# Three products of constants left out of the routing stage of a two-layer decoder kernel

## The chip, the core and the metric

The kernel runs on one core of a Trainium2 chip. The metric is device microseconds (us) of one execution, from the runs shown below; lower is better. TensorE is the matmul engine (PE in the profile, and PEld for its weight loads), VectorE is DVE, ScalarE is ACT, GpSimd is POOL, and SyncE (SP) issues most of the transfers.

## The reference

Two decoder layers on 256 tokens of width 1024, all in float32. Layer 0 has sparse attention over keys that an indexer picks, then a dense SwiGLU. Layer 1 has stick-breaking attention, then a mixture of experts: each token goes to the best two of eight experts. Only the last part bears on this case:

```python
def moe_ffn(u, router_w, w_gate_up, w_down):
    B, S, D = u.shape
    tok = u.reshape(B * S, D)
    logits = (tok @ router_w).astype(jnp.float32)
    top_vals, top_idx = lax.top_k(logits, TOP_K_EXPERTS)          # 2 of 8
    gates = jax.nn.softmax(top_vals, axis=-1)
    dense_gates = jnp.sum(jax.nn.one_hot(top_idx, N_EXPERTS, dtype=jnp.float32) * gates[..., None], axis=1)
    y = jnp.zeros_like(tok)
    for e in range(N_EXPERTS):
        y = y + dense_gates[:, e:e + 1].astype(tok.dtype) * swiglu(tok, w_gate_up[e], w_down[e])
    return y.reshape(B, S, D)
```

## The kernel before

Each engine has its own program, written out by hand in order, and the engines meet at semaphores; there is no planner. The first 408 us of the profiled execution hold layer 0, the shared keys and values and the attention of layer 1. Their products are made in three passes of split operands (`product`, whose matmuls are on lines 530 to 532). Then comes the routing stage, from about 408 to 425 us, and after it the expert stage until the end.

The routing stage is a chain between TensorE, VectorE and ScalarE. TensorE transposes the residual stream `h` (`stream_T`, line 863) and multiplies it by the router's weights (`router_product`, line 870: weights of 8 columns, 128 moving columns). The logits are copied out of PSUM (ACT `routeT_act`, DVE L1916) and turned by two small transposes (line 909), the last of which sets `route_ps`. VectorE then works out which two experts each token takes: L1918 to L1931, some ten small operations, the last of which sets `sel_done`. TensorE counts with constant triangles and ones (lines 915 to 919, 8 moving columns each) the rank of each token within its expert; `rank_ps` is set by line 917 and `total_ps` by line 919. VectorE finishes the reciprocal norms (`rstd(3, t)`: L1587, ACT L1140, L1590), turns ranks to slots (L1939, L1940, L1952) and writes the pick matrix `m_pick` (L1956), which sets `e_pick`. TensorE then gathers the first expert's 96 slots (`gather_first`, line 937: 16 products with 96 moving columns), ACT and DVE copy the result into `m_u_now`, and the expert stage begins.

Between these links the kernel before has `keep_clock(n)`, which issues n products of the identity with 512 columns of constants into `bank[3]`. Two of them stand behind the transposes of line 909 and ahead of the wait for `sel_done`; one stands behind line 919 and ahead of the wait for `e_pick` in `gather_first`. Nothing reads what they write: `bank[3]` is written anew, with `start=True`, by the gather. In float32 a product is two records of the profile, so the three products are six matmul records and six weight loads, on line 877.

In the expert stage each of eight experts is one job. `expert_up` and `expert_dn` multiply its weights as they come, on tiles of 32 columns side by side (`on_third`, line 965); `hidden_T` (line 1008) transposes the hidden values. SP issues the weights (lines 456, 461 and 466) into a ring of six buffers for the first matrix and four for the second, and waits for TensorE's `up_used` and `dn_used` before it fills a buffer again.

Of the kernel before, what the change touches and what calls it, by code (L numbers as in the profile page):

```python
# [64 lines left out]
def program(nc, x, a_norm_w, a_w_in, a_q_norm_w, a_k_norm_w, a_w_out, kv_norm_w, kv_w, b_norm_w,  # L65
# [6 lines left out]
    with ctx:  # L72
        def sb(name, shape, dt=f32):
            return ctx.enter_context(nc.sbuf_tensor(name, shape, dt))
# [17 lines left out]
        cst = sb("cst", [P, K_END])  # L92
# [32 lines left out]
        ident, before, upto = cst[:, K_ID:K_ID + P], cst[:, K_BEFORE:K_BEFORE + P], cst[:, K_UPTO:K_UPTO + P]  # L125
# [87 lines left out]
        bank = [pair[i // 2][:, 512 * (i % 2):512 * (i % 2) + 512] for i in range(8)]  # L213
# [183 lines left out]
        def _(sp):  # L397
# [3 lines left out]
            def columns(n, w, *blocks):  # L401

                if n >= RING:
                    sp.wait_ge(*((up_used, 2 * (n - RING + 1)) if n - RING < T_OUT else (up_l, split_end(n - RING))))
                src = w.rearrange("(k p) c -> p k c", p=P)
                cols, at = sum(size for _, size in blocks), 0
                for c0, size in blocks:
                    sp.dma_start(up_tile(n, cols)[:, :, at:at + size], src[:, :, c0:c0 + size]).then_inc(up_in[n % RING], 16)
                    at += size
# [99 lines left out]
        def _(pe):  # L509
# [270 lines left out]
            for j in range(4):  # L780
                for half in range(2):
                    n = 2 * (T_BQ + j) + half
# [88 lines left out]
                                   start=(k == 0), stop=(k == KD - 1))  # L871
                return mm

            def keep_clock(n):

                for _ in range(n):
                    pe.matmul(bank[3], ident, cst[:, 0:512], start=True, stop=True)

            def first_half_T():
                stream_T(0, 0)  # L880
                stream_T(0, 1)
# [25 lines left out]
            for t in range(NT):  # L907
                pe.wait_ge((routeT_act, routeT_dve)[t], 1)
                mm = pe.transpose(bank[1][:, NEXP * t:NEXP * t + NEXP], route_T[:, P * t:P * t + P], ident[0:NEXP, 0:NEXP])
            mm.then_inc(route_ps, 1)  # L910
            keep_clock(2)
            pe.wait_ge(sel_done, 1)
            routed = rt[:, 5]

# [2 lines left out]
            pe.matmul(bank[6][:, 8:16], before, routed[:, 1, :], start=False, stop=True).then_inc(rank_ps, 1)  # L917
            pe.matmul(bank[1][:, 16:24], ones, routed[:, 0, :], start=True, stop=False)
            pe.matmul(bank[1][:, 16:24], ones, routed[:, 1, :], start=False, stop=True).then_inc(total_ps, 1)
            keep_clock(1)  # L920


            def slot_tokens(j):
# [170 lines left out]
        def _(act):  # L1094
# [74 lines left out]
            def proj_copy(j, t):  # L1169

                act.wait_ge(*((proj_ps, j - 1) if j < 4 and t == 0 else (up_used, 2 * j + t + 1)))
                cols = sum(size for _, size in IN_TILES[j])
                copy(in_rows[j][:, t, :], bank[(NT * j + t) % 4][:, 0:cols], rs[:, 0, t:t + 1]).then_inc(proj_sb, 1)
# [50 lines left out]
            def weights_T(g):  # L1224

                i0, n, _, ps, _ = softmax_part(g)
                act.wait_ge(probT_ps, g + 1)
                copy(probT[:, i0:i0 + n, P:], ps.rearrange("p (i s) -> p i s", i=n)).then_inc(probT_act, 1)
# [883 lines left out]
```

## Time and profile before

| | |
|---|---|
| Median of 3 runs | 1168.45 us (1167.71 to 1168.53) |
| The profiled execution | 1168.2 us, of which the span from first to last instruction is 1166.5 us |
| TensorE busy in the span | 1150.8 us (99%) |
| VectorE, ScalarE, GpSimd busy | 288.6, 284.4, 30.5 us |
| Mean granted TensorE clock | 0.999 |

The times of the rows are microseconds from the span's start. The granted clock is a share of TensorE's full 2.4 GHz: 1.00 is that rate and 0.50 is 1.2 GHz. A matmul's record covers its run through the engine, so records overlap: how fast products follow on one another is read from their starts. The profiled execution's 1168.2 us is 0.25 us below the median of the runs.

### The profile page before, as it was taken

To read this page: it belongs to the slowest core of one execution; us is meant where nothing else is said; L and a number is where in the kernel's file an instruction comes from. 1 tells how busy PE (TensorE), PEld (TensorE's weight loads), DVE (VectorE), ACT (ScalarE), POOL (GpSimd) and SP (SyncE) were. 2 spreads that over 40 slices of the span, in tenths; PEclk is the share of its full clock that TensorE was granted. 3 is DMA by queue.
4 is the path that set the end of the run, shared out by engine and by line. 5 is a ranking of instruction groups with operands and counts; after the bars stand their busy time and mean duration, and the time that the engine had idled before them with its cause. 6 is when DMAs were issued, how large, how long until landed. Compare 5 with 4: busy or idle time off the path is not lost.

```text
span 1166.5 us, 31770 instructions
## 1 busy us (share of the span) xinstructions
PE 1150.8 (99%) x14480; PEld 1008.8 (86%) x14480; DVE 288.6 (25%) x470; ACT 284.4 (24%) x476; POOL 30.5 (3%) x84
## 2 busy tenths in 40 slices
PE   9999999999999999999999999999999999999997
PEld 7768999999898888898888888888888888888885
DVE  3775654554653430000000000000000000000002
ACT  4765543443548430011001011001001001001001
POOL 0000000000000011000000000000000000000100
PEclk9999999999999999999999999999999999999999
DMA  9639965552254299989999999999999999999992
GB/s 338 226 124 287 364 206 197 192 187 91 89 201 145 101 388 390 352 317 384 376 392 394 374 393 390 363 394 396 377 384 395 384 371 394 394 366 393 389 388 98
DMA packets 174368, 361.21 MB, mean 310 GB/s; under 512 B 6616, under 2 KB 50048, under 8 KB 174240
## 3 DMA queue, kind: packets, MB, share of 16 engines
q1 hardware_dynamic: 169936, 343.78, 80.6%
q0 software_dynamic: 4080, 15.34, 3.9%
q8 instruction: 116, 1.90, 0.7%
q10 hardware_dynamic: 224, 0.09, 0.0%
q14 instruction: 12, 0.10, 0.0%
HBM read 347.65 MB, written 11.53 MB: 308 GB/s over the span
## 4 chain that ended last, share of the span: by engine, by line
PE 95%; DVE 3%; ACT 2%; issue 0%; ACTq 0%; DVEq 0%
PE pair L965 60%; PE pair L530 9%; PE pair L531 8%; PE pair L532 8%; PE pair L1008 2%; PE pair L564 1%; PE pair L590 1%; PE pair L947 0%; ACT up_hi L1102 0%; DVE up_lo L1607 0%; PE pair L629 0%; PE pair L545 0%; DVE dn_ring L1711 0%; PE pair L937 0%; PE pair L870 0%
## 5 line engine op out<-in xcount | busy, mean ns | idle before, releaser
L965 PE MATMUL pair<-up_ring,work 128*32 128x384 f32 (+1 forms) x6144 | 357.0, 380 | 0.0
L965 PEld LDWEIGHTS pair<-up_ring,work 128*32 128x32 f32 x6144 | 341.8, 110 | 10.8 <-issue 5.2
L965 PE MATMUL pair<-dn_ring,kT_a 128*32 128x256 f32 (+1 forms) x3168 | 249.6, 451 | 0.8 <-ACT kT_a L1102 0.8
L965 PEld LDWEIGHTS pair<-dn_ring,kT_a 128*32 128x32 f32 x3168 | 159.2, 110 | 61.0 <-issue 1.2
L2002 DVE TENSOR_TENSOR work<-work,pair 128x384 f32<-128x384 f32 x40 | 22.2, 554 | 524.4 <-PE pair L965 524.4
L1102 ACT ACTIVATE kT_a<-pair 128x384 f32<-128x384 f32 (+3 forms) x65 | 25.3, 402 | 488.3 <-PE pair L1008 488.2
L530 PE MATMUL pair<-uT_hi,up_hi 128*128 128x256 f32 x480 | 135.7, 283 | 2.4 <-DVE uT_lo L1621 2.3
L965 PE MATMUL pair<-up_more,work 128*32 128x384 f32 (+1 forms) x2304 | 135.8, 380 | 0.0
L531 PE MATMUL pair<-uT_lo,up_hi 128*128 128x256 f32 x480 | 135.0, 281 | 0.0
L532 PE MATMUL pair<-uT_hi,up_lo 128*128 128x256 f32 x480 | 135.0, 281 | 0.0
L1607 DVE TENSOR_TENSOR up_lo<-up_ring,up_hi 128x2048 fp32r<-128x2048 f32 x46 | 105.3, 2291 | 113.3 <-ACT up_hi L1102 113.2
L965 PEld LDWEIGHTS pair<-up_more,work 128*32 128x32 f32 x2304 | 129.3, 110 | 3.9 <-issue 2.7
L1102 ACT ACTIVATE up_hi<-up_ring 128x2048 fp32r<-128x2048 f32 x46 | 87.9, 1913 | 103.7 <-PE pair L532 98.5
L530 PEld LDWEIGHTS pair<-uT_hi,up_hi 128*128 128x128 f32 x480 | 90.5, 189 | 3.7 <-issue 2.9
L531 PEld LDWEIGHTS pair<-uT_lo,up_hi 128*128 128x128 f32 x480 | 90.6, 189 | 0.4
L532 PEld LDWEIGHTS pair<-uT_hi,up_lo 128*128 128x128 f32 x480 | 90.6, 189 | 0.0
L530 PE MATMUL pair<-up_hi,uT_hi 128*128 128x512 f32 x128 | 51.7, 404 | 1.1 <-DVE uT_lo L1630 1.1
L531 PE MATMUL pair<-up_lo,uT_hi 128*128 128x512 f32 x128 | 50.6, 395 | 0.0
L532 PE MATMUL pair<-up_hi,uT_lo 128*128 128x512 f32 x128 | 50.6, 395 | 0.0
L1413 ACT ACTIVATE work<-pair 128x384 f32<-128x384 f32 x40 | 19.7, 491 | 118.7 <-PE pair L965 118.7
L532 PE MATMUL pair<-dn_hi,hid_lo 128*128 128x512 f32 x80 | 31.6, 395 | 0.0
L531 PE MATMUL pair<-dn_lo,hid_hi 128*128 128x512 f32 x80 | 31.6, 395 | 0.0
(304 smaller groups left out, 794.2 us busy)
## 6 DMA issues: line engine op xcount, KB each, us to landing
up_ring<-in_moe_w_gate_up SPq DMA_DIRECT2D x128, 1024.0 KB, 13.2
dn_ring<-in_moe_w_down SPq DMA_DIRECT2D x88, 1024.0 KB, 14.6
up_more<-in_moe_w_gate_up SPq DMA_DIRECT2D x48, 1024.0 KB, 14.0
up_ring<-in_dense_w_gate_up SPq DMA_DIRECT2D x22, 1024.0 KB, 9.2
dn_ring<-in_dense_w_down SPq DMA_DIRECT2D x11, 1024.0 KB, 11.1
up_ring<-in_kv_w SPq DMA_DIRECT2D x4, 2048.0 KB, 8.1
y_rows<-q_T POOLq DMA_DIRECT2D x1, 6528.0 KB, 33.4
up_ring<-in_a_w_in SPq DMA_DIRECT2D x4, 1024.0 KB, 12.6
```

The lines of the kernel that those rows point to most:

```text
L530: pe.matmul(ps, a_hi, b_hi, start=start, stop=False, skip_group_check=shared)
L531: pe.matmul(ps, a_hi, b_lo, start=False, stop=False, skip_group_check=shared)
L532: return pe.matmul(ps, a_lo, b_hi, start=False, stop=stop, skip_group_check=shared)
L564: mm = pe.matmul(bank[2 * t + g][:, 0:I_HALF], uT_in[:, k, P * t:P * t + P], index_tile(half)[:, j, I_HALF * g:I_HALF * g + I_HALF], start ...
L590: mm = pe.matmul(bank[(NT * j + t) % 4][:, 0:cols], uT_in[:, k, P * t:P * t + P], up_tile(j, cols)[:, k, :], start=(k == 0), stop=(k == KD ...
L965: return pe.matmul(out, a, w, start=start, stop=stop, tile_position=(0, THIRD * place), skip_group_check=True)
L1008: mm = pe.transpose(bank[6][:, P * f:P * f + P], m_hid[:, g % GROUPS % 2, P * f:P * f + P], ident)
L1102: return act.activation(out_, in_, ACT.Copy, scale=scale)
L1413: act.activation(v, gate[:, 0:384], ACT.Silu).then_inc(e_silu, 1)
L1607: dve.tensor_tensor(buffer(up_lo, n, 2048), raw_piece(n), buffer(up_hi, n, 2048).bitcast(f32), ALU.subtract).then_inc(up_l, 1 + unsplit)
L2002: dve.tensor_tensor(v, v, bank[tile_bank[(tile + 1) % STEPS % 3]][:, 0:384], ALU.mult).then_inc(e_raw, 1)
```

## The change

The helper and its two calls are taken out. Nothing else of the kernel is touched, on any engine.

```diff
-            def keep_clock(n):
-
-                for _ in range(n):
-                    pe.matmul(bank[3], ident, cst[:, 0:512], start=True, stop=True)
-
...
             mm.then_inc(route_ps, 1)
-            keep_clock(2)
             pe.wait_ge(sel_done, 1)
             routed = rt[:, 5]
...
             pe.matmul(bank[1][:, 16:24], ones, routed[:, 1, :], start=False, stop=True).then_inc(total_ps, 1)
-            keep_clock(1)
```

## Rows read from the trace of the kernel before

**Rows 1.** The page's second part: TensorE busy, granted clock, in 40 slices.

```profile
PE   9999999999999999999999999999999999999997
...
PEclk9999999999999999999999999999999999999999
```

**Rows 2.** Chain of waits through the routing stage: start, duration, engine and line.

```profile
413.99 2.73 PE pair L870 x24
...
417.08 0.24 PE pair L909
...
418.97 0.18 DVE rt L1931
419.15 0.08 DVE rs L1587
...
419.98 0.17 DVE rs L1590
...
420.18 0.18 DVE rt L1939
...
420.96 0.58 DVE work L1956 x2
...
421.58 3.81 PE pair L937 x32
425.39 4.61 PE pair L965 x41
```

**Rows 3.** Timeline of the same stage, TensorE's records: start, duration.

```profile
417.24 1.99 PE L877 MATMUL pair<-cst 128*128 128x512 f32 x4
...
419.20 0.39 PE L915 MATMUL pair<-rt,cst 128*128 128x8 f32 x2
...
419.67 0.37 PE L917 MATMUL pair<-rt,cst 128*128 128x8 f32 x2
...
420.34 1.10 PE L877 MATMUL pair<-cst 128*128 128x512 f32 x2
```

**Rows 4.** Timelines of two short windows: starts of the third and fourth record.

```profile
418.20 1.02 PE L877 MATMUL pair<-cst 128*128 128x512 f32 x2
...
418.63 0.59 PE L877 MATMUL pair<-cst 128*128 128x512 f32 x1
```

**Rows 5.** Windows, two jobs: length; busy PE, PEld, DVE, ACT, POOL; clock, DMA share, GB/s.

```profile
471.75:563.09 91.34, 91.34 (x1483) 80.36 (x1484) 5.72 (x13) 8.36 (x20) 1.91 (x4) 1.00 0.98 355
563.09:654.42 91.33, 91.33 (x1483) 80.36 (x1484) 5.71 (x13) 8.35 (x20) 1.86 (x4) 1.00 1.05 387
```

**Rows 6.** SP's own waits between 425 and 1150 us: total, times, longest.

```profile
SPq L466 <- PE pair L965: 134.6, 33, 9.9
SPq L456 <- PE pair L965: 36.4, 7, 11.0
```

**Rows 7.** Windows of the end: length, TensorE busy (records), granted clock, DMA share, GB/s.

```profile
1156.10:1157.70 1.60, 0.00 (x0) 1.00 0.00 0
...
1164.70:1164.80 0.10, 0.00 (x0) 1.00 0.05 20
1164.80:1164.90 0.10, 0.00 (x0) 0.52 0.10 41
```

**Rows 8.** Timeline of the end: the last records of TensorE.

```profile
1159.95 1.45 PE L1074 MATMUL pair<-q_T,work 96*128 96x512 f32 x3
```

**Rows 9.** Timeline of the first microseconds, by short windows: TensorE's first products.

```profile
1.32 0.80 PE L545 MATMUL pair<-work 128*128 128x256 f32 x1 [1.32 <-DVE work L1664]
...
2.33 1.06 PE L545 MATMUL pair<-work 128*128 128x256 f32 x2
...
3.61 0.93 PE L545 MATMUL pair<-work 128*128 128x256 f32 x2
4.04 0.93 PE L545 MATMUL pair<-work 128*128 128x256 f32 x3
4.37 0.81 PE L545 MATMUL pair<-work 128*128 128x256 f32 x3
```

## The prediction

> **What bounds the kernel now.** I read the page first. TensorE is busy in every one of the 40 slices and its clock row shows full rate in all of them [rows 1]. That says which engine matters, and not what the routing stage is worth, so the next view is the chain of waits from 405 to 430 us. The reader should see it change hands. Up to the router's products it is all TensorE [rows 2]; from 417.08 us it runs through the two small transposes, VectorE and ScalarE, and at 421.58 us it comes back to TensorE with the gather. Line 877, the work that is taken out, is nowhere on it. Third, the expert stage. Two jobs that follow each other take 91.34 and 91.33 us with TensorE busy to the last hundredth [rows 5], and in the same stretch the transfer queue stood waiting for TensorE's buffers, 134.6 and 36.4 us in all [rows 6]. The weights are ahead of the engine. So whatever moves the start of the gather at 421.58 us, or slows TensorE after it, arrives at the end of the kernel undiminished: no later transfer absorbs it.
>
> **What is removed, and what the instructions themselves are worth.** Three products, which are six records: four from 417.24 us and two from 420.34 us [rows 3].
> The first four follow one another every 0.43 us (418.20 and 418.63 [rows 4]). The last of them therefore has its 512 columns in the engine by 418.63 + 0.43 = 419.06 us; its modelled end of 418.63 + 0.59 = 419.22 us includes the run out of the array, which the next product need not await. The next product, line 915, waits for VectorE's L1931, which ends at 418.97 + 0.18 = 419.15 us, and starts at 419.20 us [rows 2, 3]. The wait for VectorE ends 0.09 us later than the constants, so taking them out gives nothing. Suppose I am wrong about the run-out and line 915 could start earlier: it still cannot before 419.15 us, a gain of 0.05 us. Nor is that on the path: the rank is ready at 419.67 + 0.37 = 420.04 us [rows 3], and its reader L1939 starts at 420.18 us, after the reciprocal L1590 that ends at 419.98 + 0.17 = 420.15 us [rows 2]. VectorE's own norms set that link, with 0.11 us to spare.
> The last two records start at 420.34 us and take 0.43 us each at their input, so they are through by 420.34 + 0.86 = 421.20 us (modelled end 421.44 us), and the gather starts at 421.58 us, 0.04 us after `m_pick` is written [rows 2, 3]. Nothing is gained there either.
> As instruction time the edit is therefore worth 0, with an end of 0.1 us to the good (0.05 us at line 915 and as much for the gather's first weight load, if either was held up at all). No transfer, semaphore or wait is added or moved, and the `bank[3]` that was written has no reader. PSUM loses six accesses, while the other engines were running operations of under 0.6 us from a dependent chain; I put no gain on that.
>
> **What the engine's idleness is worth.** This is the cost that the diff hides. Without line 877 TensorE has almost nothing to stream from the last router product to the gather. The router's products end at 413.99 + 2.73 = 416.72 us; then come two transposes of 8 columns, the ten records of lines 915 to 919 with 8 moving columns each, and at 421.58 us the gather: 421.58 - 416.72 = 4.9 us with no product of more than 8 columns [rows 2]. The trace has just two stretches to set beside that. Between 1156.10 and 1157.70 us the engine had no record for 1.60 us, and the granted clock stayed at 1.00 [rows 7]. After the last product of all, which ends at 1159.95 + 1.45 = 1161.40 us [rows 8], it stayed at 1.00 until 1164.80 us and then stood at 0.52 and 0.50, its lower level [rows 7]: it fell after 3.4 us without work. The new thin stretch, 4.9 us, is longer than the one that ended in a fall, and each of its two empty parts (417.3 to 419.20 us, 1.9 us; 420.5 to 421.58 us, 1.1 us) is about as short as the one that did not. The question is whether ten products of 8 columns count for work. They stream next to nothing, so I take it that they mostly don't, and that the clock falls near the end of the stretch.
> The Trainium skill, in "TensorE: Matmul & The Clock Gate", section on HAM oscillation, has it that an engine which idles between bursts of matmuls is throttled again and starts its next burst at half rate. By the 1.60 us row the sum would stay at 1168.2 us, by that rule it would be the forecast below; the trace agrees with the rule at its end, where the fall is seen, and has no case of a fall between bursts.
>
> The price of a fall is read at the very start, where the engine begins at the lower level. The clock row reads 1.00 there too, but the records don't: starts 2.33 us, then 3.61 and 4.04 us are 0.43 us apart, while 4.37 us and the end of that group of three (4.37 + 0.81 = 5.18 us, less the 0.38 us that one of them takes) give (4.80 - 4.37) / 2 = 0.215 us [rows 9]. Products of the same shape take twice the time until about 4.2 us. The engine worked from 1.32 us to about 4.2 us, 2.9 us, at half rate, which cost it 2.9 / 2 = 1.45 us. That is the row nearest to this case: work without a pause, begun at the lower level.
> Bounds. Less: the gather's records come every 3.81 / 32 = 0.119 us [rows 2], more than their 96 columns need at 0.215 / 256 us each (0.081 us). If the weight load that fills the difference does not slow, a record takes 0.161 us at half rate, 1.35 times as long, and 2.9 us of it lose 2.9 x (1 - 1 / 1.35) = 0.75 us. And nothing, if the clock holds. More: the lower rate lasts the whole gather and it doubles, +3.81 us; if the clock has fallen before 419.20 us, the rank products, 0.84 us from 419.20 to 420.04 us, double as well and, less the 0.11 us to spare, add 0.73 us. That is +4.5 us. I take 1.45 us.
> Sum, against the profiled execution's own time: 1168.2 + 0 + 1.45 = 1169.65 us. Its time is 0.25 us below the median of the runs, so against that: **1169.9 us**.
>
> **The rivals.**
> *The clock holds.* The small products, with their ten weight loads of 128 columns, count as enough, or such a stretch does not suffice to make the clock fall. For it: 1.60 us without a record did no harm [rows 7], and no empty part of the new stretch exceeds 1.9 us. Against it: 4.9 us so thin are nowhere else in the trace before its end. Time: unchanged, 1168.45 us.
> *The clock falls and stays low through the whole gather (the other side: slower).* Place: lines 937 and the first experts' products. Because the engine leaves the low level only after work, and half-rate work starts late, the low stretch lasts past 425.39 us. Price 3.81 us, 1172.3 us. It decides once the low stretch covers 4.7 us of work, since half of that is the 2.34 us that make 0.2%. For it: in the start-up the engine had no gap in those 2.9 us, and here the low stretch can begin before 421.58 us. Against it: the gather is without a pause too.
> *The clock does not come back for long.* The expert products sit on 32-column tiles; if those did not count as work, the whole stage would double. The rows show nothing for that: it runs at 1.00 for about 730 us [rows 1]. A small chance.
> *A gain.* Removing the constants starts line 915 and the gather sooner. Worked out above, 0.1 us at most, 1168.35 us; to be faster by 0.2% it would need 2.34 us, and the whole chain from 416.72 to 421.58 us is 4.9 us.
>
> **How the numbers follow.** Short fall (1169.9 us): 0.50. Clock holds or a gain of 0.1 us: 0.30. Long fall (1172.3 us): 0.15. Clock stays low far longer: 0.03. A real gain over 0.2%: 0.02. The range takes in the first two with their bounds, from 1168.45 less 0.65 us (the lowest run is 0.74 us below the median) to 1169.9 plus 1.6 us, which is half way into the long fall: 1167.8 to 1171.5 us. About 0.2% (2.34 us) is what a measurement of this kernel can tell from no change. The short fall and the clock that holds both stay inside it, 0.80; the long falls are slower, 0.18; faster 0.02. So the forecast is a loss too small to be told, or none.
>
> **What the profile afterwards would show.** Right: no L877; VectorE's L1931 to L1956 at the same distances from the last transpose, the gather 4.5 us after it; the granted clock at about 0.5 in a stretch that starts between 419 and 422 us and lasts some 3 us; the gather's 32 records over 5 to 6 us instead of 3.81 us; each job still 91.34 us. If the gather takes 3.8 us at clock 1.00, the clock held and the rival is right. If it takes 7 us or the first products of line 965 are slow too, the long fall is. Wrong in another way: line 915 or the gather starting nearer to their releasers would show that the constants had delayed them; a job longer than 91.34 us would show something that I have not seen.

## The result and the profile after

The changed kernel takes 1171.31 us (median of 8 runs, 1170.17 to 1173.46), the kernel before beside it 1168.48 us (8 runs, 1167.60 to 1168.87). The ratio is 1.0027 with a 95% interval of 1.0019 to 1.0036. By the medians it is a loss of 2.83 us, 0.24%: small but clear, and just above the 0.2% that the prediction took for the least that can be told. The fastest run of the changed kernel, 1170.17 us, is slower than the slowest of the kernel before. The profiled execution took 1172.38 us, with a span of 1170.6 us.

The page's second part, which answers to [rows 1]:

```profile
PE   9999999999999989999999999999999999999997
...
PEclk9999999999999989999999999999999999999999
```

One slice of the clock row, the fifteenth, from about 410 to 439 us, has dropped from 9 to 8. The same slice of PE has, too. That is the routing stage. The chain of waits through it (start, duration, engine and line; the lines below the cut stand five to seven numbers lower: L904 is the former 909, L909 to L913 are 915 to 919, L1924 and L1949 are 1931 and 1956, L930 is the gather and L958 the experts' products):

```profile
414.56 2.73 PE pair L870 x24
...
417.65 0.24 PE pair L904
...
419.53 0.18 DVE rt L1924
...
421.52 0.58 DVE work L1949 x2
...
422.15 7.03 PE pair L930 x32
429.18 10.84 PE pair L958 x98
```

Read it against [rows 2] by distances, since this execution reached the stage 0.57 us later (below). From the end of the last router product (414.56 + 2.73 = 417.29 us) to the gather's start at 422.15 us are 4.86 us; before, 421.58 - 416.72 = 4.86 us. Not a hundredth of a microsecond was gained or lost in the chain. The gather's 32 records then take 7.03 us instead of 3.81 us. Three windows of TensorE, cut where the clock changes, show why (length, busy time and records, granted clock, DMA share, GB/s):

```profile
412.00:422.10 10.10, 6.93 (x55) 1.00 1.04 393
422.10:428.93 6.83, 6.78 (x32) 0.50 1.04 392
428.93:440.00 11.07, 11.07 (x204) 1.00 0.74 275
```

The granted clock fell from 2.4 to 1.2 GHz at 422.10 us, 0.05 us ahead of the gather, and stayed there for 6.83 us. All 32 records of the gather start in that stretch, the last of them at 428.87 us. The jobs of the expert stage did not slow: two that follow each other take 91.34 us each, as in [rows 5]. The first of them:

```profile
475.53:566.87 91.34, 91.34 (x1483) 80.33 (x1484) 5.71 (x13) 8.34 (x20) 1.91 (x4) 1.00 0.97 354
```

The two profiled spans differ by 1170.6 - 1166.5 = 4.1 us, of which 3.22 us are the gather. The rest lies where the change has no part. The start-up stayed at the lower clock longer and brought 0.57 us (the router's 24 records begin at 414.56 instead of 413.99 us): the first ten records, which before end at 5.18 us [rows 9], take until 1.32 + 4.55 = 5.87 us here.

```profile
1.32 4.55 PE L545 MATMUL pair<-work 128*128 128x256 f32 x10 [1.32 <-DVE work L1657]
```

And a low stretch from 1162.79 to 1166.20 us, in the last eight records' work, brought 0.27 us (from the first of these records to the end of the span, 1170.6 - 1161.56 = 9.04 us against 1166.5 - 1157.73 = 8.77 us). One of its windows:

```profile
1163.00:1164.00 1.00, 1.00 (x3) 0.50 0.00 0
```

Three further profiles of the kernel before (below) reach the router's 24 records at 414.29, 413.91 and 414.44 us: the start-up varies like this from execution to execution whatever the kernel. It is why a span or a single time is a poor judge here, and why the experiments are read by one distance within the profile: from the end of the last router product to the first expert product, 425.39 - 416.72 = 8.67 us before and 429.18 - 417.29 = 11.89 us after.

### The profile page after: what moved, and what is told of

It is laid out like the page before. It is cut to its first block, busy times and chain, and to the rows that moved or that the text cites. A ratio compares the mean times of both kernels' runs of the same rounds, so it can differ in the third digit from the quotient of the medians.

```text
span 1170.6 us, 31758 instructions
## 1 busy us (share of the span) xinstructions
PE 1153.2 (99%) x14474; PEld 1011.6 (86%) x14474; DVE 288.7 (25%) x470; ACT 284.2 (24%) x476; POOL 30.7 (3%) x84
## 4 chain that ended last, share of the span: by engine, by line
PE 94%; DVE 2%; ACT 2%; DMA 0%; issue 0%; ACTq 0%; DVEq 0%
PE pair L958 60%; PE pair L530 9%; PE pair L532 8%; PE pair L531 8%; PE pair L1001 2%; PE pair L564 1%; PE pair L590 1%; PE pair L930 1%; PE pair L940 0%; ACT up_hi L1095 0%; DMA norm_rows<-in_b_norm_w 0%; DVE up_lo L1600 0%; PE pair L629 0%; DVE dn_ring L1704 0%; PE pair L870 0%
## 5 line engine op out<-in xcount | busy, mean ns | idle before, releaser
L958 PE MATMUL pair<-up_ring,work 128*32 128x384 f32 (+1 forms) x6144 | 357.0, 380 | 0.0
L958 PEld LDWEIGHTS pair<-up_ring,work 128*32 128x32 f32 x6144 | 341.7, 110 | 10.8 <-issue 5.2
L958 PE MATMUL pair<-dn_ring,kT_a 128*32 128x256 f32 (+1 forms) x3168 | 249.7, 451 | 0.8 <-ACT kT_a L1095 0.8
L958 PEld LDWEIGHTS pair<-dn_ring,kT_a 128*32 128x32 f32 x3168 | 158.9, 110 | 61.4 <-issue 1.4
L958 PE MATMUL pair<-up_more,work 128*32 128x384 f32 (+1 forms) x2304 | 135.9, 380 | 0.0
L958 PEld LDWEIGHTS pair<-up_more,work 128*32 128x32 f32 x2304 | 129.2, 110 | 4.0 <-issue 2.7
```

What stands on the lines that cost most here:

```text
L958: return pe.matmul(out, a, w, start=start, stop=stop, tile_position=(0, THIRD * place), skip_group_check=True)
```

## The experiments

**The changed kernel again.** No edit. This run has a second profile of it; a third and a fourth come further down.

> The changed kernel once more, beside the others on the same chip, for a second profile. Theory A with a fall that is not tied to an instruction: the granted clock goes to 0.50 at another distance from the gather's start than the 0.05 us of the first profile, the low stretch has another length than 6.8 us, and the gather's 32 records take another time than 7.03 us; the run's loss against before is the gather's excess over 3.81 us, plus that of the first expert products. A rival, that the fall is set off by the engine's own waiting for the gather's pick: it comes again at the gather's start to within 0.2 us, and the gather takes 7.0 us again.

Measured: 1170.82 us (11 runs, 1169.41 to 1172.57) against 1168.41 us (30 runs, 1167.39 to 1169.16), ratio 1.0021 (1.0012 to 1.0030). In the profile the clock fell long before the gather:

```profile
412.00:419.52 7.52, 5.67 (x45) 1.00 1.03 390
419.52:429.76 10.24, 9.29 (x42) 0.50 1.04 397
```

```profile
419.78 0.59 PE L909 MATMUL pair<-rt,cst 128*128 128x8 f32 x2 [1.89 <-DVE rt L1924]
420.22 0.57 PE L910 MATMUL pair<-rt,cst 128*128 128x8 f32 x2
...
422.77 0.53 PE L930 MATMUL pair<-work,h 128*128 128x96 f32 x1 [0.70 <-DVE work L1949]
```

The first two rows are windows, the others the timeline. Here even the rank's products run at half rate, 0.44 us from pair to pair where [rows 3] has 0.23 to 0.24 us ((419.67 - 419.20) / 2), and the gather starts 422.77 - 417.30 = 5.47 us after the last router product, 0.61 us late. The fall is tied to no instruction: it came 0.05 us ahead of the gather in one execution and 3.25 us ahead in this one. From router to experts: 429.90 - 417.30 = 12.60 us, 3.93 us more than before.

**One place alone, and one product in each.** N1 and N2 are 2 and 0, then 0 and 1, then 1 and 1; 0 stands for a call that is left out.

```diff
             mm.then_inc(route_ps, 1)
-            keep_clock(2)
+            keep_clock(N1)
             pe.wait_ge(sel_done, 1)
...
-            keep_clock(1)
+            keep_clock(N2)
```

> The two products ahead of the wait for sel_done stay, the one ahead of the gather is left out. Nothing is left out of the computation. Theory A (the whole loss is TensorE work done at the lower clock, and what brings the fall is the length of the stretch with nothing but 8-column products): the stretch shrinks from 4.9 us to 421.58 - 419.06 = 2.5 us, less than the 3.4 us without work that ended in a fall at the end of the kernel before; the clock holds in the routing stage and the time is that of before, 1168.4 us, within 0.3 us. Rival B (the place before the gather is what counts, because the fall after the change came just ahead of the gather, at 422.1 us): the clock still falls in most executions and the time stays at 1171 us. Rival C (the instructions cost something themselves): a small part of the 2.8 us comes back, without a fall to be seen.

> The one product ahead of the gather stays, the two ahead of the wait for sel_done are left out. Theory A: the stretch with nothing but 8-column products is 420.34 - 416.72 = 3.6 us, as long as the one that ended in a fall, and 0.86 us of constants follow: the clock falls in some executions and not in others, the median is between, about 1169.5 us, and the runs spread over 1168 to 1172 us. Rival B: the clock holds, 1168.4 us.

> One product in each place. Theory A: the longest stretch with nothing but 8-column products is from 418.1 to 420.34 us, 2.2 us, shorter than in the variant with only the first two: the clock holds, 1168.4 us. If it is not the longest stretch but the work in the whole of the 4.9 us that counts, two products hold the clock no better than two in one place, and a third of the work less than before may let it fall in some executions: 1168.4 to 1170 us.

| products | median us (runs) | ratio, 95% interval | fall at, gather starts at | low for | router to experts |
|---|---|---|---|---|---|
| 2 and 0 | 1170.10 (11) | 1.0012 (1.0003 to 1.0021) | 423.53, 422.49 | 3.41 us | 10.30 us |
| 0 and 1 | 1171.49 (8) | 1.0026 (1.0015 to 1.0037) | 420.39, 424.08 | 6.82 us | 11.56 us |
| 1 and 1 | 1168.96 (11) | 1.0007 (0.9998 to 1.0016) | 420.72, 421.54 | 3.41 us | 9.93 us |

The clock fell in the profile of each. It does not fall in every execution, though: of the 11 runs with 2 and 0, two took 1167.45 and 1167.59 us, like the fastest of before, at a granted clock of 1.000, where a low stretch of 3.41 us alone would leave 0.9985. With two products in front and none behind it fell 1.04 us after the gather had begun:

```profile
412.00:423.53 11.53, 10.21 (x69) 1.00 1.04 397
423.53:426.94 3.41, 3.41 (x18) 0.50 1.05 388
```

So my reading by the longest empty stretch fails: 2.5 us with nothing but 8-column products was to be safe by it, and was not. Rival B, the rival that the second place is the one that counts fails as well, since its product alone saves nothing. In that variant the constants themselves fell into the low stretch, ran over, and held the gather back to 424.08 us, 6.35 us after the last router product instead of 4.86 us. So both places are needed. With one product in each the profile shows a fall and 1.26 us of loss, but the interval of the times includes 1: how often it falls in that variant is not shown.

**One product more in either place** (3 and 1; 2 and 2), the same edit.

> One product of constants more in the first place (3 and 1), nothing left out. It tests the cover that the prediction costed: the constants' columns are through by 419.06 us and the product behind them starts at 419.20 us. With one more, 2 x 0.43 us, they are through at 419.92 us, 0.72 us late, of which 0.11 us were to spare before the rank's reader. Expected by that sum: line 915 starts 0.72 us later, the gather 0.6 us later, the time is 1169.0 us, no fall in the routing stage. A rival, that the modelled ends of the records count and the cover was already overrun by 0.03 us: 0.75 us and more. Another, that the extra work costs nothing since the engine's queue takes it in: 1168.4 us.

> One product of constants more in the second place (2 and 2), nothing left out. The constants are through at 420.34 + 4 x 0.43 = 422.06 us where the gather could start at 421.58 us: the gather starts 0.48 us later, the time is 1168.9 us, no fall in the routing stage.

With 3 and 1, line 915 starts 420.86 - 417.67 = 3.19 us after the last router product, before 419.20 - 416.72 = 2.48 us: 0.71 us late, where 0.72 us were worked out. The gather is 0.61 us late, where 0.6 us were. The rows, at full clock:

```profile
418.18 2.84 PE L877 MATMUL pair<-cst 128*128 128x512 f32 x6
420.86 0.28 PE L915 MATMUL pair<-rt,cst 128*128 128x8 f32 x2
...
423.14 3.81 PE L937 MATMUL pair<-work,h 128*128 128x96 f32 x32
```

With 2 and 2 the gather is 0.55 us late (0.48 us worked out; the sum took 0.43 us for every record, but the first two of a group start 0.51 us apart, at 420.34 and 420.85 us before). So the sum that costed the cover holds: it ends where the columns are through, not at the modelled end of the records, and the two and one products of before leave it whole. By the distance from router to experts the fourth product costs less, 426.45 - 417.34 = 9.11 us against 8.67 us, 0.44 us. The gather's row with 2 and 2:

```profile
422.75 3.71 PE L937 MATMUL pair<-work,h 128*128 128x96 f32 x32
```
The medians, 1168.50 and 1168.52 us beside 1168.44 us, where 1169.0 and 1168.9 us were expected (ratios 1.0003, 0.9994 to 1.0012), are too coarse to show it; only the fastest runs, 1168.08 and 1168.14 us against 1167.44 us, do.

**Products of 8 columns in the same gaps.**

```diff
-                    pe.matmul(bank[3], ident, cst[:, 0:512], start=True, stop=True)
+                    pe.matmul(bank[3][:, 0:8], ident, cst[:, 0:8], start=True, stop=True)
...
-            keep_clock(2)
+            keep_clock(8)
...
-            keep_clock(1)
+            keep_clock(4)
```

> The constants' products stay in both gaps, but with 8 moving columns instead of 512, and 8 and 4 of them instead of 2 and 1, so that the gaps are filled with 16 and 8 records spaced by their weight loads, about 0.11 us each, through by 419.1 and 421.2 us. Nothing is left out. Theory A (products of 8 columns do not keep the clock up, the step on which the forecast of a fall rests): the clock falls as in the changed kernel, 1171 us. The rival of the prediction that small products with their weight loads of 128 columns suffice: the clock holds, 1168.4 us.

Measured: 1172.76 us (5 runs), ratio 1.0036 (1.0023 to 1.0050). The profile shows the gaps filled and the gather in time (4.87 us after the last router product), and the clock falls all the same (windows, as above):

```profile
412.00:421.12 9.12, 8.90 (x75) 1.00 1.04 395
421.12:427.94 6.82, 6.82 (x34) 0.50 1.05 393
```

TensorE counts as busy for 8.90 of the 9.12 us ahead of the fall. In the changed kernel it was 6.93 of 10.10 us. Being shown as busy was no help. These products did not hold the clock; those with 512 columns did. The prediction's step that the ten small ones don't count is borne out.

**The constants behind the wait.** The same three products, placed where they fill no gap.

```diff
             mm.then_inc(route_ps, 1)
-            keep_clock(2)
...
-            keep_clock(1)
...
                 pe.wait_ge(e_pick, 1)
+                keep_clock(3)
                 for k in range(KD):
```

> The same three products of constants, all of them behind the wait for the pick matrix, right ahead of the gather, so that they fill no gap and cover nothing: the same instructions, without the effect on the gaps. At full rate they cost 6 x 0.43 = 2.6 us by themselves. Theory A (the low stretch is what costs, whatever the work in it): the clock falls at some point from 419 to 423 us as in the changed kernel, the constants run at half rate too, and the time is before + 2.6 us + the loss of the changed kernel of 2.4 to 2.8 us, 1173.5 us. Rival D (the low stretch was long, 6.8 us in the first profile of the changed kernel, because the gather's products, spaced by their weight loads, don't bring the clock back as dense ones do): with 512-column products right behind the fall, it lasts 3 to 3.5 us each time, and the loss is 1.7 us, 1172.7 us.

Measured: 1172.26 us (5 runs), ratio 1.0038 (1.0024 to 1.0051), 3.82 us over before: 6 x 0.43 = 2.58 us of constants at full rate and 1.24 us of loss, about half of what the changed kernel loses. The profile has one low stretch of 3.42 us, from 420.84 to 424.26 us, with the constants starting at 421.40 us. Dense work behind the fall thus went with a short low stretch. One profile of it is thin ground for that. Hence two further profiles each of the changed kernel and of this variant.

> The changed kernel, for a further profile. Rival D (with the gather's products behind the fall the clock comes back late): a low stretch of 6.8 us or more again, from the last router product to the first expert product 11.5 to 12.6 us against 8.67 us before. Theory G (the length is chance, set by when the fall comes, whatever follows): low stretches of 3.4 us appear here too.

> As for the look before it: 6.8 us or more by rival D, 3.4 us among them by theory G; and the fall at yet another distance from the gather's start.

> The variant with the three products of constants behind the wait, for a further profile. Rival D: a low stretch of 3.4 us again, since dense work follows the fall. Theory G: 6.8 us or more as often as in the changed kernel.

> As for the look before it: 3.4 us by rival D, 6.8 us or more as often as in the changed kernel by theory G.

The profiles in which the clock fell in the routing stage, without the two variants that have a 512-column product in the second place, by the moment of the fall against the start of the work that follows the wait for the pick matrix (minus: ahead of it); the last column is the distance from the last router product to the first expert product, less the 8.67 us of before:

| kernel | fall against start | low for | loss in the stage |
|---|---|---|---|
| changed, fourth | +0.48 us | 3.41 us | 1.63 us |
| first place only | +1.04 us | 3.41 us | 1.63 us |
| changed, first | -0.05 us | 6.83 us | 3.22 us |
| 8 columns | -0.75 us | 6.82 us | 2.89 us |
| changed, third | -0.98 us | 6.83 us | 2.78 us |
| changed, second | -3.25 us | 10.24 us | 3.93 us |
| constants behind, first | -0.56 us | 3.42 us | 3.97 us, less 2.58 us of constants 1.39 us |
| constants behind, third | -0.31 us | 3.41 us | 4.10 us, less constants 1.52 us |
| constants behind, second | -0.49 us | 3.42 us | 4.00 us, less constants 1.42 us |

Two of the rows behind it, the fourth profile of the changed kernel and the second of the constants behind the wait:

```profile
422.36:425.77 3.41, 3.41 (x18) 0.50 1.05 390
```

```profile
421.21:424.63 3.42, 2.93 (x4) 0.50 1.03 389
```

Neither theory is right as it was put. A low stretch of 3.4 us appears in the changed kernel too, against rival D; but only in the profile in which the gather was already running when the clock fell, as in the one with 2 and 0. Where the fall came ahead of the gather, the stretch was 6.8 us or more in all four cases, and with the 512-column products in the gather's place, 3.4 us in all three. The two variants left out of the table fit in. With 1 and 1 the clock fell at 420.72 us while constants were running (from 420.20 us), and the stretch was 3.41 us though the gather began only 0.82 us later; with 0 and 1 it fell at 420.39 us, 1.85 us ahead of the constants, and the stretch was 6.82 us. So both the moment of the fall and the work that follows it go with the length, which is against theory G. These are eleven profiles; what ends a low stretch is not shown beyond that.

**Three more profiles of the kernel before.** No edit.

> The kernel before, unchanged, for another profile of it. The variant with three and one products started its gather 0.61 us later by its profile and yet its median is only 0.06 us above before's. Theory E (two products and one don't always hold the clock: in some executions of the kernel before it falls in the routing stage too, which costs about as much as the third product does): one or more of three looks has a granted clock of 0.50 between 415 and 430 us, and from the last router product to the first expert product takes over 9 us instead of 8.67 us. Rival F (the medians differ by what the start and the end of the kernel do, where the clock also changes level from execution to execution): 8.67 us in all three.

> The kernel before again, a further profile; as for the first look: a fall in the routing stage in one or more of three by theory E, none by rival F.

> The kernel before again, a third profile; as for the first look.

No fall in the routing stage, and 425.69 - 417.02 = 8.67, 425.31 - 416.64 = 8.67 and 425.83 - 417.17 = 8.66 us from router to experts; with the first profile, four of four. The chain's row of the gather at one of them:

```profile
421.88 3.81 PE pair L937 x32
```

No profile bears theory E out, and those with 3 and 1 and with 2 and 2 products show no fall in the routing stage either. That the variant with 3 and 1 is not told from before by its median then falls to the start-up and the end, which differ between executions as rival F has it; how much each adds was not measured run by run.

**Constants in the gaps at the end too.**

```diff
-            def keep_clock(n):
+            def keep_clock(n, b=3, cols=512):
...
-                    pe.matmul(bank[3], ident, cst[:, 0:512], start=True, stop=True)
+                    pe.matmul(bank[b][:, 0:cols], ident, cst[:, 0:cols], start=True, stop=True)
...
                     hidden_T(k, g)
+                if last and g == GROUPS - 1:
+                    keep_clock(1, 7, 256)
...
+                keep_clock(1, 7)
                 pe.wait_ge(e_pickT_sb, 1)
```

> The kernel before with constants in two gaps at the very end as well (a product of 256 columns where the engine waits 0.8 us for the last hidden values, one of 512 columns where it waits 1.6 us for the last expert's result). Nothing is left out. In the profiles of the changed kernel and of the variants with 3 and 1 and with 2 and 2 products the clock fell within the last 10 us and cost 0.3 to 0.5 us there; in that of before it did not. Theory: the falls at the end come from these gaps and are gone; the routing stage is as before; the median is 0.1 to 0.4 us below before's, hardly to be told. Rival: the falls at the end come from the engine's little work in the last expert tiles, the constants don't stop them, and the time is that of before or, where the constants run over, up to 0.1 us longer.

Measured: 1168.24 us (11 runs, 1167.70 to 1168.83) against 1168.80 us (15 runs, 1167.62 to 1169.33), ratio 0.9997 (0.9988 to 1.0006). If it gains anything it is less than can be told. Its profile has no low stretch among the last products, but none of the four profiles of the kernel before has one either, so whether these constants would prevent it stays open.

## Why the prediction was wrong

*What bounds the kernel, and that a loss ahead of the experts arrives whole.* Right. Each job takes 91.34 us as before; between the first expert product and the last scatter lie 1161.56 - 429.18 = 732.38 us against 732.34 us.

*The instructions are worth nothing by themselves.* Right, and shown from both sides: the chain keeps its 4.86 us without them in the first profile, and one more in either place holds the gather back by 0.61 and 0.55 us where the same sum gave 0.6 and 0.48 us. The prediction's 421.20 us for the end of the second place's columns is 0.08 us early for the reason given there, which changes nothing before 421.58 us.

*The clock falls.* Right: in all four profiles of the changed kernel, at a moment that differs. The Trainium skill's rule in "TensorE: Matmul & The Clock Gate", section on HAM oscillation, that an engine idling between bursts is throttled again, is borne out here by a fall between bursts, which the trace of before did not have. The engine was not idle throughout, but the ten small products did not prevent the fall, as the prediction assumed. Its comparison with the 3.4 us at the end, however, was no measure of safety, as two products in front showed. It was one value of several, too: in the three further profiles of the kernel before the clock fell 3.66, 4.17 and 3.12 us after the last product, and in the one with constants at the end 1.94 us after it.

*The price of a fall.* This is the step that failed, the term of 1.45 us. It took the 2.9 us of work at the lower clock from the start-up, and the ratio of two from there. The ratio was nearly right: the changed kernel's 32 records take 7.03 us against 3.81 us, a factor of 1.85, and in the middle of the gather they start every 0.213 us against 0.112 us, a factor of 1.9. The weight loads slow as well (median 333 ns, before 185 to 193 ns), which rules out the lower bound's 0.161 us. The length was wrong. The low stretch lasted 3.41, 6.83, 6.83 and 10.24 us in the four profiles, and the routing stage lost 1.63, 2.78, 3.22 and 3.93 us, 2.9 us on average, twice the forecast; the medians say 2.8 and 2.4 us. The start-up was the wrong neighbour. There the engine goes on from its first product with 256-column products that follow each other without a gap, while here the clock fell ahead of the gather in three of four profiles, and in the first of them the stretch ran through all of it. The variant with dense work behind the wait, 3.4 us three times, shows that such work goes with a short stretch. And the 2.9 us were the low end of what the start-up itself does: the records turn to the closer spacing at about 4.2 us in some profiles, at 5.7 us in the first of the changed kernel and at 7.4 us in the one with 0 and 1 products. By the prediction's own sum that is 1.4 to 3.0 us, of which it had seen one value.

*The rivals and the chances.* The rival on the other side, a low stretch through the whole gather with a bound of 3.81 us and 0.73 us more if the rank products fall into it, is nearly what three of four profiles show; in the second of them the rank products fell into it and cost 0.61 us. It had the mechanism and nearly the price (1172.3 us) and was given 0.15. Its argument was in the text, that the low stretch can begin before 421.58 us, and was set aside by the remark that the gather is without a pause too, which says nothing on what comes before it. "The clock holds" never happened in the changed kernel's profiles, and none of its 19 timed runs was as fast as the slowest run of before beside it. So the time, 1171.31 us, lies in the range but near its upper end, and the sign, slower by more than 0.2%, had only 0.18 against 0.80 for a loss too small to tell. That it lies inside is luck in part: the prediction calls the upper end of 1171.5 us half way into the long fall, but half way from 1169.9 to 1172.3 us is 1171.1 us.

## What to carry to other kernels

Work whose result nobody reads can be worth its place where the engine's clock is at stake: cost it by what the clock does behind it, not by its instructions. Price a fall by the stretch it will cover, from the earliest moment at which it can come through all the work that follows at the lower rate, and not by the start-up. When a span varies by a microsecond from run to run for reasons elsewhere, read the effect as a distance between two instructions on either side of the change.

## What the runs showed of the hardware

The clock's changes of level are not tied to the program: the same instructions saw a fall at 419.52, 420.61, 422.10 and 422.36 us. The low stretches in the routing stage came in few lengths, 3.4, 6.8 and 10.2 us. The clock can fall late in the kernel as well, among the last eight records: in four of the 18 profiles (the changed kernel's first two, 3 and 1, 2 and 2), from 1162.79 to 1166.20 us in the first of them. The profile's clock column reads 1.00 in the first microseconds, while the products' spacing there is that of the lower level [rows 9]; there the records are to be trusted and not the column. And a TensorE shown busy for 98% of the time (8.90 of 9.12 us) had its clock taken down.
